# Layer norms run by two halves of the tokens across the stage boundary, and the engine loops written out, in a two-layer hybrid decoder

## What is computed

```python
for l in range(DEPTH):
    x = layer_norm(ALPHA * x + 0.5 * swiglu(x, ffn1_w_in[l], ffn1_w_out[l]), ...)        # norm 0
    x = layer_norm(ALPHA * x + mixer(x), ...)                                            # norm 1
    x = layer_norm(ALPHA * x + memory_cross_attn(x, mem, xa_w_q, xa_w_kv, xa_w_o), ...)  # norm 2
    x = layer_norm(ALPHA * x + 0.5 * swiglu(x, ffn2_w_in[l], ffn2_w_out[l]), ...)        # norm 3
# layer_norm: (x - mean) / sqrt(var + EPS) * g + b;  swiglu: (silu(x @ w_gate) * (x @ w_up)) @ w_out, D_FF = 2816
```

## Time and profile before

| | |
|---|---|
| median of 3 runs (lowest to highest) | 2421.01 us (2413.27 to 2421.06) |
| span of the profiled execution | 2417.9 us |
| mean granted TensorE clock | 0.958 of full |
| busy, share of the span | PE 94%, PEld 78%, DVE 46%, ACT 32%, POOL 43% |
| instructions | 29435 |

### The profile page before, as it was taken

The page is one execution under the profiler, slowest core; times in us unless marked ns, Lnnn a source line. Parts: engine busy times, 40 slices in busy tenths (PEclk is TensorE's granted clock), DMA queues, the critical chain, the costliest instruction groups (busy, mean ns, idle before and its releaser), DMA issues.

```text
span 2417.9 us, 29435 instructions
## 1 busy us (share of the span) xinstructions
PE 2277.5 (94%) x10280; PEld 1875.0 (78%) x10280; DVE 1109.0 (46%) x1137; ACT 779.6 (32%) x1017; POOL 1051.2 (43%) x434
## 2 busy tenths in 40 slices
PE   7999998968999899999999999988789998999996
PEld 5888887856878788888778888877568887888885
DVE  2333335786654633333343333359766455333333
ACT  3222223625354322222142222245344433222223
POOL 5444444413462544444354444443245624444441
PEclk9999998978999899999999999989789998999998
DMA  4223321210341222232222232222112312222320
GB/s 159 95 95 100 108 89 61 93 41 28 117 140 44 70 96 97 99 110 95 77 88 96 95 108 96 83 69 70 48 66 96 131 53 70 95 95 95 113 95 35
DMA packets 54074, 212.49 MB, mean 88 GB/s; under 512 B 6000, under 2 KB 6256, under 8 KB 53744
## 3 DMA queue, kind: packets, MB, share of 16 engines
q1 hardware_dynamic: 52704, 207.64, 25.6%
q10 hardware_dynamic: 1296, 3.90, 0.5%
HBM read 209.42 MB, written 2.10 MB: 87 GB/s over the span
## 4 chain that ended last, share of the span: by engine, by line
PE 41%; issue 36%; POOL 20%; POOLq 1%; ACT 0%; DVE 0%; ACTq 0%; DMA 0%; DVEq 0%; SPq 0%
POOL w_lo L341 18%; PE psum L429 12%; PE psum L430 12%; PE psum L433 12%; POOL act_lo L366 2%; PE psum L465 1%; POOL act_lo L394 1%; PE psum L409 1%; PE psum L469 1%; PE psum L410 1%; PE psum L411 1%; PE psum L487 1%; PE psum L445 0%; PE psum L511 0%; POOLq L339 0%
## 5 line engine op out<-in xcount | busy, mean ns | idle before, releaser
L341 POOL TENSOR_TENSOR w_lo<-raw,w_hi 128x1024 fp32r<-128x1024 f32 (+3 forms) x356 | 952.2, 2677 | 1248.6 <-ACT w_hi L838 1248.5
L838 ACT ACTIVATE w_hi<-raw 128x1024 fp32r<-128x1024 f32 (+3 forms) x356 | 401.6, 1129 | 1395.4 <-PE psum L433 1311.3
L429 PE MATMUL psum<-act_hi,w_hi 128*128 128x512 f32 x1836 | 727.4, 396 | 40.9 <-ACT w_hi L838 40.9
L430 PE MATMUL psum<-act_lo,w_hi 128*128 128x512 f32 x1836 | 722.6, 394 | 0.0
L433 PE MATMUL psum<-act_hi,w_lo 128*128 128x512 f32 x1836 | 453.9, 389 | 0.0
L429 PEld LDWEIGHTS psum<-act_hi,w_hi 128*128 128x128 f32 x1836 | 349.9, 191 | 121.6 <-ACT w_hi L838 47.0
L430 PEld LDWEIGHTS psum<-act_lo,w_hi 128*128 128x128 f32 x1836 | 350.2, 191 | 73.7 <-issue 0.5
L433 PEld LDWEIGHTS psum<-act_hi,w_lo 128*128 128x128 f32 x1836 | 344.7, 188 | 72.1
L1233 DVE TENSOR_TENSOR work<-work,psum 128x512 f32<-128x512 f32 x88 | 60.6, 689 | 616.1 <-PE psum L433 565.6
L429 PE MATMUL psum<-h_hi,w_hi 128*128 128x512 f32 x704 | 275.7, 392 | 0.0
L430 PE MATMUL psum<-h_lo,w_hi 128*128 128x512 f32 x704 | 275.5, 391 | 0.0
(11 more groups left out here) (227 smaller groups left out, 2103.6 us busy)
## 6 DMA issues: line engine op xcount, KB each, us to landing
raw<-w_in SPq DMA_DIRECT2D x176, 512.0 KB, 3.2
raw<-w_out SPq DMA_DIRECT2D x64, 704.0 KB, 4.0
raw<-w_mix SPq DMA_DIRECT2D x36, 512.0 KB, 3.3
raw<-w_kv SPq DMA_DIRECT2D x32, 512.0 KB, 3.2
raw<-w_mixout SPq DMA_DIRECT2D x16, 576.0 KB, 3.7
raw<-w_q SPq DMA_DIRECT2D x16, 512.0 KB, 3.3
raw<-w_o SPq DMA_DIRECT2D x16, 512.0 KB, 3.2
raw<-w_v SPq DMA_DIRECT2D x4, 768.0 KB, 4.2
```

Source lines behind the costliest of these rows:

```text
L341: nc.gpsimd.tensor_tensor(w_lo[:, r, 0:width], raw[:, j, 0:width], w_hi[:, r, 0:width].bitcast(F32), ALU.subtract).then_inc(slot_split, 1)
L429: nc.tensor.matmul(o, hi, b_hi, start=start and k == 0, stop=False)
L430: nc.tensor.matmul(o, hi, b_lo, start=False, stop=False)
L838: A(w_hi[:, place % SPLIT, 0:width], raw[:, place, 0:width], ACT.Copy).then_inc(w_hi_made, 1)
```

## The change

Norms 0, 2 and 3 (`BY_HALVES`) are run for tokens 0 to 255 (half a) and 256 to 511 (half b). The last output tile of a feed-forward, and the last two of the attention's output, are multiplied half by half: all slots for a, then all for b in another PSUM bank, every matmul 256 columns wide, and the statistics and `bcast` of a stand between b's matmuls. The first pair of slots of the next stage (`first_pair_by_halves`) is multiplied for a, then for b, 96 matmuls of 256 columns, with b's statistics and `bcast` inside a's part. DVE, ACT and POOL work on pairs of x tiles, 2 x 256 columns an instruction, except ACT's `affine`, which is two instructions of 256. The scalars are spread by full float32 matmuls against twice the identity, so the two DVE operations that split them go. ACT makes the high parts of the next stage's first two slots inside the norm, loads the table for silu after each such norm (before: only after norms 2 and 3), and makes the first two slots' high parts at the kernel's start before it makes x's; `split_first` is gone. The last norm writes no high part, and stores its output by halves in eight DMAs. The hardware loops of all engines are written out; `decay_rates` moves from the first two steps of the feed-forward to its fifth and sixth. In outline (indentation cut, removed code left out):

```diff
+BY_HALVES = (True, False, True, True)
+WHOLE = (KT - 1, KT, KT - 2, KT - 1)
...
@@ sync
...
+    for h in range(2):
+        for k in range(0, KT, 2):
+            sp.wait_ge(x_finished, h * KT + k + 2)
+            sp.dma_start(out[:, k:k + 2, HALVES[h]],
+                         x[:, k:k + 2, HALVES[h]]).then_inc(out_stored, 16)
+    sp.wait_ge(out_stored, 128)
...
@@ gpsimd
...
+    def split(layer, s):
+        n = layer * SLOTS + s
+        pool.wait_ge(w_hi_made, n + 1)
+        width = slot_width(s)
+        nc.gpsimd.tensor_tensor(w_lo[:, n % SPLIT, 0:width], raw[:, n % RAW, 0:width],
+                                w_hi[:, n % SPLIT, 0:width].bitcast(F32),
                                 ALU.subtract).then_inc(slot_split, 1)
...
+    def split_x(layer, n, h, k):
+        cols = HALVES[h]
+        pool.wait_ge(x_hi_made, x_count(layer, n, k + 1, h))
+        nc.gpsimd.tensor_tensor(act_lo[:, k:k + 2, cols], x[:, k:k + 2, cols],
+                                act_hi[:, k:k + 2, cols].bitcast(F32),
+                                ALU.subtract).then_inc(x_split, 2)
...
+    def after_norm(layer, s, x_layer, n):
+        split(layer, s)
+        split_x(x_layer, n, 0, 0)
+        split(layer, s + 1)
+        for h in range(2):
+            for k in range(0 if h else 2, KT, 2):
+                split_x(x_layer, n, h, k)
...
@@ tensor
...
+        a, b = HALVES
+        hi_ready(layer, s)
+        x_hi(0, 0)
+        for k in range(2):
+            hi_by_hi(0, k, a, start=k == 0)
+        slot_ready(layer, s)
+        for k in range(2):
+            lo_by_hi(0, k, a)
+        stats_rest(x_layer, n, 1)
+        hi_ready(layer, s + 1)
+        for k in range(2):
+            hi_by_hi(1, k, a, start=k == 0)
+        for k in range(2, KT, 2):
+            if k == KT - 2:
+                bcast(x_layer, n, 1)
+            x_hi(0, k)
+            for u in range(k, k + 2):
+                hi_by_hi(0, u, a)
+                lo_by_hi(0, u, a)
+                hi_by_hi(1, u, a)
+            x_lo(0, k - 2)
+            for u in range(k - 2, k):
+                hi_by_lo(0, u, a)
+        slot_ready(layer, s + 1)
+        for k in range(KT):
+            lo_by_hi(1, k, a)
+        x_lo(0, KT - 2)
+        for k in range(KT - 2, KT):
+            hi_by_lo(0, k, a)
+        for k in range(0, KT, 2):
+            x_hi(1, k)
+            for u in range(k, k + 2):
+                hi_by_hi(0, u, b)
+                lo_by_hi(0, u, b)
+                hi_by_hi(1, u, b)
+                hi_by_lo(1, u, a)
+            if k:
+                x_lo(1, k - 2)
+                for u in range(k - 2, k):
+                    hi_by_lo(0, u, b)
+        for k in range(KT):
+            lo_by_hi(1, k, b)
+        x_lo(1, KT - 2)
+        hi_by_lo(0, KT - 2, b)
+        hi_by_lo(0, KT - 1, b, stop=True).then_inc(slot_multiplied, 1)
+        for k in range(KT):
+            last = hi_by_lo(1, k, b, stop=k == KT - 1)
+        last.then_inc(slot_multiplied, 1)
...
+    def stats_rest(layer, n, h):
+        rest = range(WHOLE[n], KT) if BY_HALVES[n] else range(KT - 1, KT)
+        part = rest[0] + len(rest) * (h + 1) - 1
+        pe.wait_ge(z_added, z_count(layer, n, part))
+        for m in rest:
+            column_sums(n, h, 0, x[:, m, :], False, False)
+        pe.wait_ge(z_squared, z_count(layer, n, part))
+        for m in rest:
+            last = column_sums(n, h, 1, zsq(m), False, m == KT - 1)
+        last.then_inc(stats_ready, 1)
...
+    def bcast(layer, n, h):
+        t0, t1 = tokens_in(n, h)
+        pe.wait_ge(twice_made, 1)
+        pe.wait_ge(scalars_made, group(layer, n, h))
+        for a in range(2):
+            for t in range(t0, t1):
+                c = SC0[h] + 16 + a * (t1 - t0) + t - t0
+                last = nc.tensor.matmul(scale_bank(n, h, a)[:, (t - t0) * P:][:, 0:P],
+                                        small[:, c:c + 1].to_broadcast([P, P]),
+                                        twice[:, :], start=t == t0 and (
+                                            a == 0 or not BY_HALVES[n]),
+                                        stop=t == t1 - 1 and (
+                                            a == 1 or not BY_HALVES[n]))
+        last.then_inc(bcast_ready, 1)
...
+        o = psum[:, m % 2, a]
+        hi_ready(layer, s)
+        hi_passes(0, 0, FT // 2, o, a)
+        slot_ready(layer, s)
+        lo_passes(0, o, a)
+        stats_first(layer, n, 0)
+        stats_first(layer, n, 1)
+        hi_ready(layer, s + 1)
+        hi_passes(1, 0, FT // 2, o, a)
+        slot_ready(layer, s + 1)
+        lo_passes(1, o, a).then_inc(half_done, 1)
+        o = psum[:, 3, b]
+        hi_passes(0, 0, 6, o, b)
+        stats_rest(layer, n, 0)
+        hi_passes(0, 6, FT // 2, o, b)
+        lo_passes(0, o, b).then_inc(slot_multiplied, 1)
+        hi_passes(1, 0, 4, o, b)
+        bcast(layer, n, 0)
+        hi_passes(1, 4, FT // 2, o, b)
+        lo_passes(1, o, b).then_inc(slot_multiplied, 1)
+        if layer == LAYERS - 1 and f == 1:
+            stats_rest(layer, n, 1)
+            bcast(layer, n, 1)
...
+        for m in range(KT - 2, KT):
+            pe.wait_ge(z_added, z_count(layer, 2, m - 2))
+            hi_ready(layer, S_AO + m)
+            half_hi(m, psum[:, m % 2, a], a)
+            slot_ready(layer, S_AO + m)
+            half_lo(m, psum[:, m % 2, a], a).then_inc(half_done, 1)
+        stats_first(layer, 2, 0)
+        half_hi(KT - 2, psum[:, 2, b], b)
+        stats_rest(layer, 2, 0)
+        half_lo(KT - 2, psum[:, 2, b], b).then_inc(slot_multiplied, 1)
+        stats_first(layer, 2, 1)
+        half_hi(KT - 1, psum[:, 3, b], b)
+        bcast(layer, 2, 0)
+        half_lo(KT - 1, psum[:, 3, b], b).then_inc(slot_multiplied, 1)
...
@@ scalar
...
+    def w_hi_of(n):
+        if n >= SPLIT:
+            act.wait_ge(slot_multiplied, n - SPLIT + 1)
+        if n < TOTAL:
+            act.wait_ge(raw_loaded[n % RAW], (n // RAW + 1) * 16)
+            width = slot_width(n % SLOTS)
+            A(w_hi[:, n % SPLIT, 0:width], raw[:, n % RAW, 0:width],
+              ACT.Copy).then_inc(w_hi_made, 1)
...
+    def scaled_pair(layer, n, h, k):
+        cols = HALVES[h]
+        affine(layer, n, k, cols)
+        last = affine(layer, n, k + 1, cols)
+        if n == 3 and layer == LAYERS - 1:
+            last.then_inc(x_finished, 2)
+            return
+        act.drain()
+        A(act_hi[:, k:k + 2, cols], x[:, k:k + 2, cols], ACT.Copy).then_inc(x_hi_made, 2)
...
+    def scaled_by_halves(layer, n, next_s, square_b):
+        root(layer, n, 0)
+        w_hi_of(next_s)
+        scaled_pair(layer, n, 0, 0)
+        w_hi_of(next_s + 1)
+        square_b()
+        scaled_pair(layer, n, 0, 2)
+        root(layer, n, 1)
+        silu_table()
+        scaled_pair(layer, n, 0, 4)
+        scaled_pair(layer, n, 0, 6)
+        for k in range(0, KT, 2):
+            scaled_pair(layer, n, 1, k)
...
+        for i in range(FT):
+            w_hi_of(s0 + 2 * i + SPLIT)
+            if i >= 2:
+                act.wait_ge(h_made, base + i - 1)
+            A(work[:, i % 2, :], bank(2 * (i % 2)), ACT.Silu).then_inc(gate_silu, 1)
+            w_hi_of(s0 + 2 * i + 1 + SPLIT)
+            if f == 0 and i in (4, 5):
+                decay_rates(layer, i - 4)
+        sqrt_table()
...
@@ vector
...
+    def scalars(layer, n, h, eps):
+        w = 2 if BY_HALVES[n] else 4
+        mean, sq, var, std, r, mr = (small[:, SC0[h] + c:SC0[h] + c + w]
+                                     for c in (0, 4, 8, 12, 16, 16 + w))
+        dve.wait_ge(stats_ready, group(layer, n, h))
+        V.tensor_copy(mean, psum[:, 6 + h, 0:w])
+        dve.drain()
+        V.tensor_tensor(sq, mean, mean, ALU.mult)
+        dve.drain()
+        V.tensor_tensor(sq, psum[:, 6 + h, w:2 * w], sq, ALU.subtract)
+        dve.drain()
+        V.tensor_scalar(var, sq, 0.0, eps, ALU.max, ALU.add).then_inc(var_ready, 1)
+        dve.wait_ge(std_ready, group(layer, n, h))
+        V.reciprocal(sq, std)
+        dve.drain()
+        V.tensor_tensor(sq, sq, var, ALU.mult)
+        dve.drain()
+        V.tensor_tensor(sq, sq, std, ALU.add)
+        dve.drain()
+        V.reciprocal(r, sq)
+        dve.drain()
+        V.tensor_tensor(mr, mean, r, ALU.mult).then_inc(scalars_made, 1)
...
+    def centered_pair(layer, n, h, k):
+        cols = HALVES[h]
+        if k == 0:
+            dve.wait_ge(bcast_ready, group(layer, n, h))
+        r, mr = (scale_bank(n, h, a).rearrange("p (a s) -> p a s", a=1).to_broadcast(
+            [P, 2, HALF]) for a in range(2))
+        V.tensor_tensor(x[:, k:k + 2, cols], x[:, k:k + 2, cols], r, ALU.mult)
+        dve.drain()
+        V.tensor_tensor(x[:, k:k + 2, cols], x[:, k:k + 2, cols], mr,
+                        ALU.subtract).then_inc(y_centered, 2)
...
+    def norm_by_halves(layer, n, eps, added_b):
+        scalars(layer, n, 0, eps)
+        centered_pair(layer, n, 0, 0)
+        added_b()
+        centered_pair(layer, n, 0, 2)
```

(67 more changed lines are left out.)

491 lines of the change are left out of this document (214 added, 277 removed).

## The result

The changed kernel takes 2443.38 us (median of 4 runs, 2441.71 to 2449.32) against 2421.03 (2413.27 to 2421.21): 1.0104 times the time before, with a 95% interval of 1.009 to 1.0119. It is slower by 1%, and 2 us beyond the upper end of the forecast range. The profiled execution took 2449.32 us, the slowest of the four (its mean granted clock is 0.959, that of the other three 0.961 to 0.963).

What follows compares the result with a forecast made beforehand. TensorE, busy 94% of the span, was taken as the bound, with ACT and DVE pacing what follows the norms' waits. Terms of -1.2 + 2.7 + 4.6 - 3.2 + 4.0 = +6.9 us gave 2428 us, range 2405 to 2441.

Steps and rivals of the forecast that it cites:

- The sum: Whole kernel: -1.2 + 2.7 + 4.6 - 3.2 + 4.0 = +6.9 us, giving 2428 us.
- PE's step: TensorE's time per wide matmul, taken as 0.2276 us in loops and straight code alike; a change in it would refute the forecast.
- The hole in the last tile: Feed-forward's last tile: 1.6 us waiting plus 1.8 of one-column records; clock fall taken as 1.0 in four places, +4.
- slower by the hole: Rival: each of four last tiles pays the full 3.1 us instead of 1.0, giving 2436 us; chance 0.25.
- The feed-forward boundaries: Norm 0 twice, norm 3 of layer 0: front gains spent behind, at half clock +0.9 each, +2.7 us.
- Norm 2: Attention's end: second pair of slots at 42.3 against 39.96 us with the clock halved, +2.3, twice: +4.6.
- The end: Last norm, without drain or high part: DVE's 1.36 us sets the pace, last affine at 35.0 against 38.2: -3.2.
- The start: Kernel's start: POOL no longer copies the first two slots, one copy leaves the path to its L353: -1.2 us.
- The cover is real: Rival: ACT's pairs go at 1.41, table load and `bcast` overlap, PE ends last; a third of -58 gives 2401 us; chance 0.13.
- Straight code pays: Rival: dropping about 70 loop turns of TensorE's engine saves at most 0.1 us each, 7 us, giving 2421 us; chance 0.03.

Runs made afterwards that it cites:

- a2: The changed kernel with 384 bytes of unused SBUF a partition ahead of the region of h, q, k, v and the mixer's tiles: 2424.12 us, ratio 1.0025.
- b1: The changed kernel with `bcast` of half b ahead of the pair (0,4) instead of behind it: 2418.70 us, ratio 1.0017 to the kernel before.
- d1: The changed kernel with 448 unused bytes, so the region from h on starts where the kernel before has it modulo 512 bytes: 2429.86 us, ratio 1.0041.
- a4: The kernel before with all 14 hardware loops written out and nothing else: 2417.79 us, ratio 0.9995.
- b4: The changed kernel with `bcast` of b earlier, the table load behind the norm's last pair, and the last tile's first sums later: 2412.33 us, ratio 0.9979.
- e1: The kernel before with 64 unused bytes in front of w_hi, moving weights and the region from h on, activations staying: 2452.38 us, one run.

## Why the prediction was wrong

Three steps failed: a term was put at nothing (the place of the buffers, 8.1 us), the fall of the clock behind the wait in the last tile was priced too low (4.0 for 10.8), and so was the chain of b's scalars at the boundaries (7.3 for 17.8, norm 2 included).

- **The sum** left out a term: where the buffers lie. "Straight code" and "PE's step" were looked at, but only as a mean over two streams, and the sizes of `small` and `twice` in the diff were costed at nothing. This is +8.1 us.
- **The hole in the last tile** was seen in the right place: 1.6 us of waiting for L1367 were forecast, and the timeline has 1.48 of idle time in front of L588. The fall of the clock after it was taken as 1.0 and cost 1.5 at the first boundary (16 narrow matmuls at 0.213 instead of 0.117 us) and about 3.1 at the other three places, 10.8 instead of 4.0. The rival "slower by the hole" had the right price in three of four; it was given 0.25. That the fall was 6.8 us long in three places is this trace's: a2, b1 and d1, with the same wait, have 3.4 or none at each place.
- **The feed-forward boundaries** without the hole cost 2.9, 2.8 and 3.1 us instead of 0.9: 4.44 - 1.5, 5.94 - 3.1 and 6.20 - 3.1. The step that failed is the length of b's scalar chain, not its place. DVE began it at 25.7 after the tile's start, 24.2 without the hole's 1.5, and the forecast had 24.1. But from there to the end of ACT's root it took 2.5 us instead of 1.3. Two of DVE's small operations took 0.81 and 0.93 us instead of the 0.16 of their neighbours, and both end with the POOL instruction beside them (L380 from 387.15 for 2.37, L394 from 389.48 for 1.28). The 1.4 us that they lost passed through root, table load, pair (0,4) and `bcast`; it is so at all three boundaries. The other 0.6 or so of the miss is spread: `bcast` ended 3.8 behind the high part of (0,4) instead of 3.5, and the second pair came 0.3 later behind the last high part. Of the Trainium skill, SBUF — State Buffer (SBUF: two separate sides) tells of a port pair that VectorE and GpSimd hold in turn for a whole instruction; the ends in this trace agree for L1381, whose two inputs both lie in SBUF. That L1385, with one input, ended with POOL's instruction too is the trace's. Beyond that the part worked: an ACT pair each 1.68 us (forecast 1.70), the last high part over at 43.6 and the second pair 3.9 behind it (forecast 3.6: 40.4 and 44.0).
- **Norm 2** cost 4.5 instead of 2.3, twice: +9.0. The same two operations of DVE took 0.47 and 0.93 us there, and the clock was already down for 3.4 us from 822.2, among b's matmuls of the last tile, which the forecast had at full rate.
- **The end** was forecast at -3.2; the last tile's start to the span's end shrank by 0.3 with 3.1 for the hole in it, so -3.4: right. **The start** gave -3.0 instead of -1.2, and not for the reason given: the written-out loops bring the first load forward, which a4 shows alone (-3.3). The forecast had put them at nothing by looking at PE only. The copy that POOL no longer makes brought nothing at the stage's end: h begins at 254.99 in the change and at 254.76 in a4, which still makes it.
- **The sum, measured:** -3.0 + 8.8 + 9.0 - 3.4 + 10.8 + 8.1 = 30.3 us, against 29.6 between the two spans. The stages in between make up the small rest. Without the rate of h and with fewer falls of the clock this is d1's 0.41%, 10 us. That it lies near the 6.9 forecast is luck in part: in d1's trace the five boundaries cost 18.7 us, hole included, where the forecast had 10.3, and a better start (-2.7) and a faster stretch through layer 1's mixer (3.2 less) hide part of that.
- **"The cover is real"** was half right as a possibility: with the order of b4 the halves do pay, but 2.5 us a feed-forward boundary, not a third of 10.9, and at norm 2 not reliably: its two boundaries take 42.53 and 39.15 us in b4's trace, against 39.96 before; ACT's pairs at 1.68 us remain the pace, as the forecast said. **"Straight code pays"** fell by a4.

## What to carry to other kernels

Read the start-to-start step for each streamed tile on its own, and write down how far each lies from the weights that are loaded beside it: here scratch tiles longer by 64 bytes cost as much as the clever part of the change could bring, and 64 bytes in another place 1.3%. When a wait is broken into two halves, list for every in-order engine what stands in front of the second half's scalars, and place the spreading matmul right behind them; a table load ahead of the pairs was paid in full (1.5 us a boundary). A stretch in which TensorE waits and does one-column matmuls can cost as much behind it, at the lower clock, as in it (1.5 or 3.1 us behind a wait of 1.5 here), or nothing. When two kernels differ by a few us, compare their stretches too, since a stage whose code no edit touched moved by 4 to 5.

## What the runs showed of the hardware

- The time of one fp32r matmul of 512 columns depends on where its streamed tile begins relative to the weights being loaded, modulo 256 bytes: 0.2267, 0.2289, 0.2333, 0.2333 us at 0, 64, 128, 192. Of the Trainium skill, TensorE: Matmul & The Clock Gate (Step-by-step: what each phase is for) has two independent read ports of SBUF, so that loading the next weights takes no bandwidth from the running matmul. For the time of these matmuls the measurement decides otherwise: e1 moves only the split weights and what lies behind them, by 64 bytes, and loses 31 us. Why the distance counts no run shows.
- A DVE operation on two columns took up to 0.93 us instead of 0.16 beside POOL, and ended with POOL's instruction, at the one place of the boundary where it was on the path.
- Writing the loops out brought the first weight load forward by 3.3 us and left TensorE's step at 0.2289.
- The same wait of TensorE in a dense stretch (1.48 us, then 1.92 of one-column matmuls) was followed by 6.8, 3.4 or no us at the lower clock level, in kernels that differ elsewhere.
